# Streaming encoder layer on one core: the weight of each expert step computed on ScalarE, and the layer's own TensorE work cut into pieces over its slots

## The reference

```python
h = rmsnorm(x, g_mix); proj = h @ w_in                 # 1024 -> 4*512 (q,k,v,g) + 3*512 (B,C,h)
o = rms_scale(retention(rotary(q), rotary(k), v)) * silu(g)
c = B * short_conv(C * h)                              # 3 taps
x = x + concat([o, c]) @ w_out
q = (rmsnorm(x, g_ffn) @ wq).reshape(T, 8, 2, 128)     # 8 heads, two halves
v1, i1 = top_k(q[:, :, 0] @ keys1.T, 16); v2, i2 = top_k(q[:, :, 1] @ keys2.T, 16)
top_s, e = top_k(v1[..., :, None] + v2[..., None, :], 16)   # e: expert numbers, 16 per head
act = gelu(einsum('td,thkd->thk', xn, u_tab[e]))            # u rows: 1024 floats each
x = x + einsum('thk,thkd->td', softmax(top_s) * act, v_tab[e])
y = rmsnorm(x, g_final)
```

## Time and profile before

| | |
|---|---|
| median of 3 runs | 3299.9 us (3294.3 to 3301.84) |
| profiled execution, its own time | 3302.18 us |
| its span, first to last instruction | 3300.4 us |
| DMA, whole span | 1223.47 MB, mean 371 GB/s |
| of this gathers (q0) | 1107.36 MB, 83.4% of the 16 engines' span |
| other transfers (q1) | 113.80 MB, 9.1% |
| first gather issued | 199.4 us |
| mean granted TensorE clock | 0.813 of full speed |

### The profile page before, as it was taken

How to read it: one execution, slowest core, us unless ns; L and a number is a source line. 1 busy time by engine, 2 the same in 40 slices (tenths; PEclk the granted TensorE clock), 3 DMA queues, 4 the chain that set the end, 5 groups by cost and what they waited for, 6 DMA issues and landing times.

```text
span 3300.4 us, 36101 instructions
## 1 busy us (share of the span) xinstructions
PE 2423.8 (73%) x12644; PEld 1993.6 (60%) x12644; DVE 2141.7 (65%) x6141; ACT 1607.1 (49%) x2626; POOL 1176.6 (36%) x1060
## 2 busy tenths in 40 slices
PE   8867787787776777787776887777766766667766
PEld 7656666656665666666665666655555655555555
DVE  1368875557888644556888744555788888555554
ACT  1135544455455544455455544456455455564455
POOL 0022333344443443334444333234443443444332
PEclk9978888797878888787878999888877777666666
DMA  6269998899999999899999999899999999999997
GB/s 238 79 255 358 375 374 328 310 403 402 415 387 416 383 420 394 317 388 401 418 395 414 369 421 408 320 340 373 419 403 374 366 384 367 412 417 421 421 421 320
DMA packets 183318, 1223.47 MB, mean 371 GB/s; under 512 B 21088, under 2 KB 26400, under 8 KB 43616
## 3 DMA queue, kind: packets, MB, share of 16 engines
q0 software_dynamic: 152064, 1107.36, 83.4%
q1 hardware_dynamic: 31072, 113.80, 9.1%
HBM read 1216.23 MB, written 4.86 MB: 370 GB/s over the span
## 4 chain that ended last, share of the span: by engine, by line
PE 39%; DVE 24%; DMA 18%; ACT 15%; issue 4%; POOL 0%; SPq 0%; DVEq 0%; ACTq 0%; POOLq 0%
DMA ring<-in_uv,idx 17%; PE expert_sum L813 14%; DVE ring L1094 10%; ACT ring L610 8%; PE mm L760 7%; PE mm L669 5%; PE mm L675 5%; PE x_ps L729 3%; DVE pairs_left L977 1%; ACT L621 1%; ACT dots L621 1%; DVE top_i L986 1%; DVE top_i L976 1%; PE tp L770 1%; DVE top_v L984 1%
## 5 line engine op out<-in xcount | busy, mean ns | idle before, releaser
L813 PE MATMUL expert_sum<-ident_sb,ring 128*128 128x128 f32 x8448 | 1486.3, 337 | 827.4 <-ACT ring L610 814.7
L474 POOL DMA_INDIRECT ring<-in_uv,idx x1056 | 1176.4, 1114 | 2094.6 <-PE expert_sum L813 1831.5
L813 PEld LDWEIGHTS expert_sum<-ident_sb,ring 128*128 128x128 f32 x8448 | 1235.1, 175 | 1086.2 <-ACT ring L610 1033.9
L1094 DVE CUSTOM_DVE_ANT_0 ring<-ring,xn 128x1024 f32<-128x1024 f32 x1056 | 1288.4, 1220 | 462.9 <-DMA ring<-in_uv,idx 454.5
L610 ACT ACTIVATE ring<-ring,weights 128x1024 f32<-128x1024 f32 x1056 | 1197.5, 1135 | 0.0
L621 ACT ACTIVATE dots<-dots 128x1 f32<-128x1 f32 x1056 | 211.5, 200 | 1065.2 <-DVE dots L1094 1061.9
L1076 DVE TENSOR_TENSOR weights<-dots,gate 128x1 f32<-128x1 f32 x1056 | 166.0, 157 | 166.5 <-ACT dots L621 166.2
L669 PE MATMUL mm<-stream,xn_in 128*128 128x256 f32 (+1 forms) x1024 | 255.6, 407 | 6.2 <-DVE xn_in L848 6.2
L760 PE MATMUL mm<-turn,stream 128*128 128x256 f32 (+1 forms) x1024 | 256.7, 407 | 0.7 <-ACT turn L554 0.7
L669 PEld LDWEIGHTS mm<-stream,xn_in 128*128 128x128 f32 (+1 forms) x1024 | 198.0, 199 | 47.8 <-DVE xn_in L848 6.6
L760 PEld LDWEIGHTS mm<-turn,stream 128*128 128x128 f32 x1024 | 204.8, 205 | 36.4 <-ACT turn L554 1.1
(11 more groups left out here) (158 smaller groups left out, 1541.7 us busy)
## 6 DMA issues: line engine op xcount, KB each, us to landing
stream<-in_w_ret SPq DMA_DIRECT2D x32, 1024.0 KB
stream<-in_wq SPq DMA_DIRECT2D x32, 1024.0 KB
stream<-in_w_conv SPq DMA_DIRECT2D x24, 1024.0 KB
ring<-in_uv,idx POOLq DMA_INDIRECT x1056
w_out_sb<-in_w_out SPq DMA_DIRECT2D x1, 4096.0 KB, 16.1
x<-in_x SPq DMA_DIRECT2D x8, 512.0 KB
out_y<-xn SPq DMA_DIRECT2D x8, 512.0 KB
xn_in<-in_xT SPq DMA_DIRECT2D x24, 128.0 KB
```

What stands on the lines that cost most here:

```text
L474: pool.indirect_dma_start(ring[:, g % RING, :], None, uv, bass.IndirectOffsetOnAxis(ap=rows, axis=0)).then_inc(landed[g % RING], 16)
L813: ins = pe.matmul(expert_sum[:, c * P:(c + 1) * P], ring[:, g % RING, D + c * P:D + (c + 1) * P], ident_sb[:, :], is_transpose=True, start ...
L1094: dve.tensor_tensor_reduce(u, u, xn[:, t % 3, :], 1.0, 0.0, ALU.mult, ALU.add, dots[:, g % RING:g % RING + 1]).then_inc(dotted, 1)
```

## The change

The step: DVE's `weigh` is gone. ACT computes the weight itself, by a second small activation with the gate as its scale, and scales the v half in the same step, not in the next one. The waits for the gate move from DVE to ACT with it.

The slots: a use's 8 matmuls are spread over three slots (3, 3, 2), a head's 16 over eight slots (2 in each), and the retention products and the turn over more slots. The copies out of PSUM that follow stand 4 slots behind the start of a use (before 1) and 9 behind the start of a head (before 2). Uses now come every 4 slots (before every 4.5 for the retention units of two tiles, every 3 of three tiles, every 3.5 for the convolution units); every start is derived from the last one. In the last group the heads come every 15 slots (before 21), and the sample tile's choices follow after those of tiles 6 and 7, from scores kept in `qkvg`. Norm pieces and the loads start some slots earlier.

```diff
@@ -42,12 +42,9 @@
 RANK = {t: r for r, t in enumerate(t for order in ORDERS for t in order)}
 FIRST = -2 * STEPS
 LAST = TOTAL + 16
-N_AT = 6
-RET_AT, RET_EVERY = 20, 9
-CONV_AT, CONV_EVERY = 92, 3.5
-MIX_AT, MIX_EVERY = 94, 18
-OUT_AT, OUT_EVERY = 138, 12
-QUADS_AT = 7 * STEPS + 8
+USE_AT, USE_EVERY = 24, 4
+MIX_EVERY = 22
+QUADS_AT = 7 * STEPS + 40
 
 
 def rows_of(t):
...
@@ -74,23 +71,49 @@
     return ORDERS[group_of(t)].index(t)
 
 
-def turn_at(j, r):
-    return base_of(j) + OUT_AT + OUT_EVERY * len(GROUPS[j]) + 2 * r
+def conv_at(j):
+    return base_of(j) + USE_AT + USE_EVERY * RET_UNITS * len(GROUPS[j])
+
+
+def mix_at(t):
+    j = group_of(t)
+    return conv_at(j) + (24 if j in (1, 2) else 4) + MIX_EVERY * place(t)
+
+
+def out_at(t):
+
+    j = group_of(t)
+    return max(mix_at(t) + 22, conv_at(j) + USE_EVERY * CONV_UNITS + 2 + 10 * place(t))
+
+
+def turn_at(t):
+    j = group_of(t)
+    return out_at(ORDERS[j][-1]) + 12 + 3 * place(t)
...
 def head_at(j, h):
     if j == 0:
-        return 13 * h - 18
-    return turn_at(j, len(GROUPS[j])) + 2 + (15 if len(GROUPS[j]) == 2 else 21) * h
+        return 13 * h - 26
+    return turn_at(ORDERS[j][-1]) + 5 + 15 * h
...
 def choose_at(j, h, i):
-    return head_at(j, h) + 5 + 7 * i
+
+    if GROUPS[j][i] == SAMPLE:
+        return choose_at(j, PH - 1, i - 1) + 7 * (h + 1)
+    return head_at(j, h) + 13 + 7 * i
+
...
+def score(j, h, i):
+
+    return PH * GROUPS[j][0] + h * len(GROUPS[j]) + i
 
...
 def pick(j, h, i):
 
-    return PH * GROUPS[j][0] + h * len(GROUPS[j]) + i
+    if GROUPS[j][i] == SAMPLE:
+        return PH * SAMPLE + h
+    return PH * GROUPS[j][0] + 2 * h + i
 
 
...
@@ -98,9 +121,9 @@
     out = []
     for u in range(RET_UNITS):
         for i, t in enumerate(GROUPS[j]):
-            out.append(("ret", u, t, base_of(j) + RET_AT + RET_EVERY * u + RET_EVERY * i // len(GROUPS[j])))
+            out.append(("ret", u, t, base_of(j) + USE_AT + USE_EVERY * (u * len(GROUPS[j]) + i)))
     for v in range(CONV_UNITS):
-        out.append(("ChB"[v % 3], v, None, base_of(j) + CONV_AT + int(CONV_EVERY * v)))
+        out.append(("ChB"[v % 3], v, None, conv_at(j) + USE_EVERY * v))
     return out
 
 
...
-GATES = sorted((j, last, i, first) for j in range(4) for i, t in enumerate(GROUPS[j]) for first, last in batches_of(t))
+GATES = sorted(((j, last, i, first) for j in range(4) for i, t in enumerate(GROUPS[j]) for first, last in batches_of(t)),
+               key=lambda b: pick(*b[:3]))
...
+        def scores_of(t, h):
+            if t < SAMPLE:
+                return scores[:, :, :]
+            return qkvg[:, 0, h * 2 * NK:(h + 1) * 2 * NK].rearrange("p (s k) -> p s k", s=2)
...
                 if kind == "wq":
-                    return head_at(j, n) + 1, queried, 2 * (PH * j + n + 1)
+                    return head_at(j, n) + 7, queried, 2 * (PH * j + n + 1)
                 q = use_at(j, "ret", n, GROUPS[j][-1]) if kind == "ret" else use_at(j, "ChB"[(2 * n + 1) % 3], 2 * n + 1)
-                return USES[j][q][3], projected, USES_BEFORE[j] + q + 1
+                return USES[j][q][3] + 2, projected, USES_BEFORE[j] + q + 1
...
@@ -497,7 +528,7 @@
                 for q, (kind, unit, t, slot) in enumerate(USES[j]):
                     if kind not in ("ret", "C"):
                         continue
-                    yield slot + 1
+                    yield slot + 4
...
@@ -557,20 +588,21 @@
 
             def queries(j):
                 for h in range(PH):
-                    yield head_at(j, h) + 2
+                    yield head_at(j, h) + 9
                     act.wait_ge(queried, 2 * (PH * j + h + 1))
-                    wait(act, keyed, pick(j, h, 0))
+                    wait(act, keyed, score(j, h, 0))
                     if width(j) <= 2 * P:
                         act.activation(qT[:, :], mm[:, 0, :], ACT.Copy).then_inc(query_copied, 1)
                     else:
                         for s in range(2):
                             act.activation(queryT(j, s), query_bank(j, s), ACT.Copy).then_inc(query_copied, 1)
                     for i, t in enumerate(GROUPS[j]):
-                        n, c = rows_of(t), pick(j, h, i)
-                        yield choose_at(j, h, i) - 1
+                        n, c = rows_of(t), score(j, h, i)
+                        yield head_at(j, h) + 12 + 7 * i if t < SAMPLE else head_at(j, h) + 15
                         act.wait_ge(keyed, c + 1)
-                        wait(act, scores_read, c)
-                        act.activation(scores[0:n, :, :], tp[0:n, c % 2, 0:2 * NK].rearrange("p (s k) -> p s k", s=2),
+                        if t < SAMPLE:
+                            wait(act, scores_read, pick(j, h, i))
+                        act.activation(scores_of(t, h)[0:n, :, :], tp[0:n, c % 2, 0:2 * NK].rearrange("p (s k) -> p s k", s=2),
                                        ACT.Copy).then_inc(keyed_copied, 1)
 
             def exponentials(j):
...
-
-            def scale(g):
-                act.wait_ge(weighed, g + 1)
-                v = ring[:, g % RING, D:2 * D]
-                act.activation(v, v, ACT.Copy, scale=weights[:, g % RING:g % RING + 1]).then_inc(scaled, 1)
...
@@ -619,10 +646,20 @@
                 act.wait_ge(dotted, g + 1)
                 d = dots[:, g % RING:g % RING + 1]
                 act.activation(d, d, ACT.Gelu_apprx_tanh).then_inc(gelu_done, 1)
-                if g:
-                    scale(g - 1)
+                t, k = tile_of(g)
+                if t == SAMPLE:
+                    if k == 0:
+                        act.wait_ge(quads_gate, QUADS)
+                elif k % TOPK == 0:
+                    act.wait_ge(gate_ready, gates_ready(t, k // TOPK))
+                act.wait_ge(gelu_done, g + 1)
+                w = weights[:, g % RING:g % RING + 1]
+                act.activation(w, d, ACT.Copy,
+                               scale=gate[:, 1 if t == SAMPLE else t % 4, k:k + 1]).then_inc(weighed, 1)
+                act.wait_ge(weighed, g + 1)
+                v = ring[:, g % RING, D:2 * D]
+                act.activation(v, v, ACT.Copy, scale=w).then_inc(scaled, 1)
                 advance(programs, g)
-            scale(TOTAL - 1)
             for slot in range(TOTAL, LAST + 1):
                 advance(programs, slot)
...
                         for k in range(KC):
+                            yield slot + k // 3
                             ins = pe.matmul(bank[0:n, 0:UNIT], xnj[:, k, at:at + n], weight[:, k, :],
                                             start=(k == 0), stop=(k == KC - 1))
                     else:
                         if unit % 2 == 0:
                             item = item_in("conv", j, unit // 2).rearrange("p (u k n) -> p u k n", u=2, k=KC)
                         for k in range(KC):
+                            yield slot + k // 3
                             ins = pe.matmul(bank[:, 0:w], item[:, unit % 2, k, :], xnj[:, k, :],
                                             start=(k == 0), stop=(k == KC - 1))
...
-                yield at + 8
+                yield at + 9
...
                 for h in range(H):
+                    yield at + 9 + h
                     v = vg_of(t)[0:n, h * P:(h + 1) * P]
...
                 for h in range(PH):
                     for s in range(2):
-                        yield head_at(j, h) + s
+                        yield head_at(j, h) + 4 * s
...
                         for k in range(KC):
+                            yield head_at(j, h) + 4 * s + k // 2
                             ins = pe.matmul(query_bank(j, s), weight[:, s, k, :], xnT_of_group(j)[:, k, :],
                                             start=(k == 0), stop=(k == KC - 1))
                         ins.then_inc(queried, 1)
                     for i, t in enumerate(GROUPS[j]):
-                        n, c = rows_of(t), pick(j, h, i)
-                        yield choose_at(j, h, i) - 2
+                        n, c = rows_of(t), score(j, h, i)
+                        yield head_at(j, h) + 10 + 7 * i if t < SAMPLE else head_at(j, h) + 13
                         pe.wait_ge(query_copied, copied_heads(j, h))
                         if c >= 2:
...
-                    yield USES[j][qh][3] + 1
...
+                    yield USES[j][qh][3] + 4
...
-                    yield USES[j][qb][3] + 1
+                    yield USES[j][qb][3] + 4
...
-                for h in range(PH):
-                    for i, t in enumerate(GROUPS[j]):
-                        n, c, at = rows_of(t), pick(j, h, i), choose_at(j, h, i)
+                pairs_of_tiles = [(h, i) for h in range(PH) for i in range(2)]
+                if SAMPLE in GROUPS[j]:
+                    pairs_of_tiles += [(h, 2) for h in range(PH)]
+                for h, i in pairs_of_tiles:
...
-                            best16(tv[:, s, :], ti[:, s, :], scores[0:n, s, :], left[0:n, s * NK:(s + 1) * NK],
```

(17 more changed lines are left out.)

83 lines of the change are left out of this document (44 added, 39 removed).

## The result

The changed kernel takes 3104.57 us (median of 4 runs, 3103.07 to 3105.73) against 3300.87 us (3294.3 to 3303.3) of the kernel before on the same chip: a ratio of 0.9408, interval 0.9392 to 0.9424. The direction was right; the forecast gain was less than half of the measured one.

The account below looks back on a forecast made before the run. DMA engines were taken as the bound in two stretches, coupled stalls idling them elsewhere. Terms -50 - 19 - 17 + 4 = -82 gave 3220 for the profiled execution, 3218 us as median; range 3160 to 3275.

Parts of the forecast that it names:

- This takes nothing off a step where DMA sets the pace: Every step: scaling starts 2.0 us earlier, but no time gained where DMA sets the pace; queue 2 us deeper at a stall.
- I use the second: Choice of the byte measure, against 406 GB/s: 148 us can be got back, rather than 99 us by DMA share.
- The parts taken of each term: Shares of the byte gap expected back: 80% convolution and retention (-50), 55% out and turn (-19), 70% last choices (-17).
- the eight stretches: Stretches between 199 and 2791 us with DMA share 0.86 to 0.97, whose gaps against 406 GB/s sum to 148 us.
- The retention stretches: Convolution and retention, 510 to 635, 1268 to 1389 and 2021 to 2145 us: 80% of 62 us back, -50.
- 2511 to 2791: The last choices: DVE called the bound, busy 238.73 of 280 us; 70% of 24.8 us back, -17.
- The first stretch: 199 to 510 us: +9 for PE waiting on weight loads at six places, -5 for other waits gone; net +4.
- The mechanism of the stalls: At convolution units, a producer's burst and a reader one slot behind stop all five engines in turn; DVE stands 6.62 us.
- PE as the bound: First rival: PE waits for its one PSUM bank and becomes the bound, +144 us, time 3399; chance 0.07.
- The weight loads decide: Second rival: six full load waits in the first stretch, half of two other gains, time 3261; chance 0.17.
- All back: Third rival: all 148 us come back, the first stretch too, time 3152; chance 0.17.
- What would show it: Signs: scaling 0.55 us behind dot, retention DMA share 0.97 or more, unit and head waits nearly gone, tile 0 near 3.2.

## Why the prediction was wrong

- **"This takes nothing off a step where DMA sets the pace": true, but it was applied to the wrong steps, and this is the step that failed.** Under tile 7 it holds (pace 2.51 before and after). In the layer stretches DMA didn't set the pace: 943 of 2651 us had two gathers or fewer in flight. There the step alone was worth 154 us, and I gave it no term, only the remark that the queue is 2 us deeper when a stall comes.
- **"I use the second", 406 GB/s as the full rate: failed.** It was read from 816 to 1268, which I called full for its share of 1.00. The last row had 417, and the rates above reach 420. Over 199 to 2791 the gap is 2592 x (1 - 382/420) = 235 us and not 148. In a stretch with three in flight the share is 1.00 at 402 GB/s. The Trainium skill (Perfetto Trace Analysis, Identifying the Most-Contended Engine) calls the occupancy of 16 DMA engines misleading and asks for the rate instead; the trace agrees, 0.94 at 361 GB/s. The Trainium skill (Perfetto Trace Analysis, Roofline) gives about 435 GB/s for the engines of one core running alone and some 120% of 358 in practice, 430; the rows show 420.
- **The parts taken of each term, 80, 55 and 70%: too small, and this weighs more than the 406.** Against 420 the eight stretches that my sum prices lack 190 us. My own parts of that would have given some 107 in place of 82; 186 came back, nearly all. The other 45 or so of the 235 lie in stretches that I had called full, and 5 of them came back. The retention stretches gave 106 for 50. That is more than their own gap of 73, since loads lie in other steps now (16.6 MB of them lay in these three before, 11.7 do now). In 2511 to 2791 I had called DVE the bound; 27 us came back, at 419 GB/s, with DVE busy 223.59 of 253 us.
- **The first stretch, +4: right where the loads are tight, wrong around it.** I had put +9 on the six places between slots 32 and 78. Steps 32 to 63 became 12 us slower. In their 275 to 391 us only 2.7 gathers are in flight, and PE waits for `stream`, as it never did in these steps before:
```profile
PE mm L707 <- DMA stream<-in_w_ret: 26.5, 4, 8.2
```
That is 6.6 us a place, where I had 5.6. With the new step, the kernels with the old slots take 2.96 to 2.98 us a step there, those with the new slots and 8 ring places 3.36 to 3.69. No run parts the loads from the closer spacing of the uses. What failed is the -5 for all else in the stretch: it was -31.
- **The mechanism of the stalls** **was right**, a burst and a reader one slot behind it, but the cure was the reader's place and not the pieces: bursts with late readers are no slower.
- **Costs of the weight: 0.295 us, not 0.20** (ACT's group of 1056 below). The kernel before had a nearer row than the gelu, an activation with a pointer as its bias at 0.29 (second line below). The Trainium skill (ScalarE: Activation LUTs, What ACT_TABLE_LOAD costs) gave 0.28 and was nearer too. It made no difference to the sum, as I had said. The Trainium skill (ScalarE: Activation LUTs, Rules for kernel authors) puts a plain multiply on VectorE. The instruction itself is shorter there (0.157), but without the lag it makes DVE wait in every step (+138 us under the new slots); with the lag the two places differ by 3 us.
```profile
L657 ACT ACTIVATE weights<-dots,gate 128x1 f32<-128x1 f32 x1056 | 311.1, 295 | 38.5 <-ACT dots L648 0.4
```
```profile
1500.15 0.29 ACT L549 ACTIVATE stat<-stat,eps_sb 128x1 f32<-128x1 f32 x1
```
- **The rivals.** PE as the bound fell: group 2 has a share of 1.02 at a clock of 0.92. "The weight loads decide" fell as a whole, though steps 32 to 63 show its mechanism. "All back", 3152, was nearest; its doubt ("dependent chains one slot apart remain") cost nothing that shows, and it stopped short for the 406: with the 190 us that the eight stretches lack against 420 it would have said about 3110.
- **What would show it**: the scaling 0.55 us behind the dot's end (0.6 measured), the share above 0.97 came true, the waits for DVE's units nearly went (85.8 to 4.6), those of ACT fell to about a quarter. Under tile 0 the pace was neither the 3.2 us of the forecast nor under the 2.9 of "all back" throughout: 2.67 at steps 0 to 31, 3.62 at 32 to 63, 2.8 at 64 to 127.

What stays open: why the rate falls with few in flight beyond the idle share, that is why packets take longer then. And the 9 us ahead of the first gather: it was issued at 187.9 to 191.1 us in the kernels with pieces in the prologue, but at 197.2 in the one of them with early readers, at 193.3 and 194.6 with bursts and late readers, and at 196.5 to 201.3 with the old slots. Both pieces and late readers seem to help there; this was not taken apart.

## What to carry to other kernels

- Before calling a stretch DMA-bound, count the steps in which the consumer waits for its row (here 144 of 161 where it was, 52 of 161 where it wasn't). A busy share near 1 says little; the rate, the wait count and the number of transfers in flight say it.
- When engines work in lock step through in-order queues, look at what stands between an operation and its consumer in each queue. A lag of one step, a reader one slot too early and a producer one slot too late are the same fault: taking the lag out gave 154 us of 3300, PE one slot ahead 174, readers two slots later 91. Such cures don't add.
- A wait per step on a second engine (0.5 us here) can cost more than the shorter instruction saves. Try an operation where its input is made.

## What the runs showed of the hardware

- The rate of indirect gathers of 1 MB goes with how many are in flight (counted as above, kernel before): 284 GB/s at one, 361 at two, 402 at three, 417 or 418 from four on, and up to 420 in the changed kernel. With 4 ring places, in a stretch without stalls, 2.0 in flight gave 334.
- An ACT activation of 128x1 took 0.20 us with a fixed scale and 0.295 with a pointer as its scale; the same product on DVE 0.157.
- TensorE's granted clock was 0.65 to 0.96 of full speed in the stretches of the changed kernel, 0.76 to 0.94 with layer work, whether the work came in pieces (0.83 over the run) or in bursts (0.82).
